# Openings of both gather streams in a two-block transformer kernel: the first head's gates and dots at once, the rest of the opening beside the picks

## The reference, cut to what matters

```python
x = x + g1 * y
h = rmsnorm(x, norm_ffn[layer]) * (1.0 + sc2) + sh2
x = x + g2 * peer_ffn(h, w_q, sub_keys, u, v)

def peer_ffn(h, w_q, sub_keys, u, v):
    q = (h @ w_q).reshape(T, 8, 2, 128)               # 8 heads, two halves each
    s = einsum('thpd,pnd->thpn', q, sub_keys)         # 128 keys per half
    top_s, top_i = top_k(s, 16)
    cand_s = top_s[:, :, 0, :, None] + top_s[:, :, 1, None, :]
    cand_i = top_i[:, :, 0, :, None] * 128 + top_i[:, :, 1, None, :]
    best_s, best_j = top_k(cand_s.reshape(T, 8, -1), 16)
    experts = take_along_axis(cand_i, best_j)         # 8 x 16 = 128 rows per token
    gates = softmax(best_s)
    act = gelu(einsum('cd,ced->ce', h, u[experts]))   # a dot of h with each row of u
    return einsum('ce,ced->cd', gates * act, v[experts])
```

## Time and profile before

| what | us |
|---|---|
| median of 3 runs | 2341.18 |
| the runs | 2337.76 to 2343.08 |
| the profiled execution | 2340.63 |
| its span | 2338.9 |

### The profile page before, as it was taken

The page is one execution under the profiler, slowest core; times in us unless marked ns, Lnnn a source line. Parts: engine busy times, 40 slices in busy tenths (PEclk is TensorE's granted clock), DMA queues, the critical chain, the costliest instruction groups (busy, mean ns, idle before and its releaser), DMA issues. The chain is left out here.

```text
span 2338.9 us, 24802 instructions
## 1 busy us (share of the span) xinstructions
PE 1892.6 (81%) x9231; PEld 1014.7 (43%) x9231; DVE 1337.5 (57%) x3278; ACT 326.9 (14%) x822; POOL 556.5 (24%) x568
## 2 busy tenths in 40 slices
PE   6998666666679799998877777799999988777776
PEld 4665333333357464444333222375655443232222
DVE  3633000000055658768877876657587678778866
ACT  1052000000021420110000000123310100000001
POOL 1000000000000114443434343200144444344332
PEclk9999888888889899999999999999999999999999
DMA  9987999999997369999999999897599999999997
GB/s 399 424 261 279 429 428 429 429 431 429 426 327 325 144 272 372 421 421 421 421 418 415 421 413 422 354 374 294 206 405 422 421 421 419 421 418 421 410 421 321
DMA packets 119160, 894.80 MB, mean 383 GB/s; under 512 B 18460, under 2 KB 30588, under 8 KB 31868
## 3 DMA queue, kind: packets, MB, share of 16 engines
q0 software_dynamic: 73728, 536.90, 55.5%
q1 hardware_dynamic: 45308, 356.25, 37.5%
HBM read 889.68 MB, written 3.42 MB: 382 GB/s over the span
## 5 line engine op out<-in xcount | busy, mean ns | idle before, releaser
L2038 PE MATMUL psum<-sb_area 128*128 128x512 f32 x2048 | 978.5, 615 | 233.5 <-DVE sb_area L2793 229.3
L2819 DVE CUSTOM_DVE_ANT_0 sb_area<-sb_area 128x1024 f32<-128x1024 f32 x512 | 626.1, 1224 | 273.0 <-DMA sb_area<-in_peer_uv,sb_peer_e 270.5
L852 POOL DMA_INDIRECT sb_area<-in_peer_uv,sb_peer_e x512 | 538.8, 1052 | 999.0 <-PE psum L2038 718.7
L2038 PEld LDWEIGHTS psum<-sb_area 128*128 128x128 f32 x2048 | 375.0, 193 | 715.8 <-DVE sb_area L2793 369.1
L1688 PE MATMUL psum<-sb_area 128*32 128x256 f32 x2048 | 172.3, 510 | 130.6 <-DMA sb_area<-in_moe_w_gu 128.0
L2321 DVE COPY sb_area<-psum 128x128 f32<-128x128 f32 x32 | 9.3, 292 | 392.0 <-PE psum L1700 392.0
L1270 ACT ACTIVATE sb_small<-sb_small 128x2 f32<-128x2 f32 x258 | 52.5, 203 | 1140.5 <-DVE sb_small L2819 1140.5
L2793 DVE SCALAR_TENSOR_TENSOR sb_area<-sb_ident,sb_small,sb_area 128x128 f32<-128x128 f32 x512 | 156.7, 347 | 50.2 <-ACT sb_small L1270 45.5
L1387 PE MATMUL psum<-sb_area 128*128 128x256 f32 x784 | 175.3, 385 | 3.5 <-DVE sb_area L2155 3.2
L1688 PEld LDWEIGHTS psum<-sb_area 128*32 128x32 f32 x2048 | 82.6, 145 | 219.6 <-DMA sb_area<-in_moe_w_gu 142.5
L829 POOL TENSOR_SCALAR_AFFINE_SELECT sb_area<-sb_area 128x256 f32<-128x256 f32 x1 | 0.4, 406 | 728.0 <-DVE sb_area L2625 728.0
(11 more groups left out here) (376 smaller groups left out, 1370.2 us busy)
## 6 DMA issues: line engine op xcount, KB each, us to landing
sb_area<-in_moe_w_gu SPq DMA_DIRECT2D x30, 4096.0 KB, 33.5
sb_area<-in_ada_w SPq DMA_DIRECT2D x72, 1024.0 KB, 12.3
sb_area<-in_moe_w_dn SPq DMA_DIRECT2D x32, 2048.0 KB, 24.1
sb_area<-in_peer_w_q_runs SPq DMA_DIRECT2D x8, 2048.0 KB, 10.0
sb_area<-in_sb_w_in_runs SPq DMA_DIRECT2D x6, 2048.0 KB, 19.7
sb_area<-in_odd_w_in_runs SPq DMA_DIRECT2D x6, 2048.0 KB, 11.4
sb_area<-in_even_w_in_runs SPq DMA_DIRECT2D x5, 2048.0 KB, 12.0
sb_area<-in_moe_w_gu SPq DMA_DIRECT2D x4, 2048.0 KB, 20.7
```

The lines of the kernel that those rows point to most:

```text
L852: pool.indirect_dma_start(uv_rows[s], None, rows, bass.IndirectOffsetOnAxis(ap=peer_e[:, m:m + 1], axis=0)).then_inc(named(f"uv_loaded{s}" ...
L2038: last = pe.matmul(ps[:, 4 + 2 * t + half, :], diag[:, m % RING, :], uv_rows[s][:, D + half * HALF:D + (half + 1) * HALF], start=(k == 0), ...
L2819: dve.tensor_tensor_reduce(uv_rows[s][:, 0:D], uv_rows[s][:, 0:D], h_tok[:, m // P, :], 1.0, 0.0, ALU.mult, ALU.add, dots[:, m % BODY:m % ...
```

## The change

Both layers now open in the same way, by one list of places:

- `find_picks` for head 0 is followed by the gates of head 0 alone, and the dots begin. Head 1 makes 5 steps before the first dot (`OPENING_STEPS`) and two steps after each dot up to pick 11, its gates after that.
- The second tile's norm moves beside the picks in `peer0` too, as it was in `peer1`: square sums on ACT after the gelus of pick 3, the variance at pick 5, the root at pick 7, the transposes at pick 8, `low_rows` at pick 10.
- Group 1's products for tile 0 stand behind the `weigh`s of picks 0 to 3, a quarter behind each, and group 0's for tile 1 at picks 12 to 19. Everything behind them moves by 4 picks.
- The keys are turned between the first two products of group 0, and the first key scores stand earlier. The output projection's remaining products stand behind the second part of the key scores in `peer1`, and before the turned tokens in `peer0`.
- Seven slots are used in the first 28 picks of both layers. The eighth joins at pick 28.
- In the whole stream a search now starts at pick 12 of a unit (14 in the first) and makes two steps per dot for the first eight picks, then one; the exponential of its gates stands at pick 22 instead of 26.
- Gates and their sums lie in other memory, and `peer1` has its own diagonal matrices for the first 8 picks.

```diff
-SEARCH_AT = 8
-EXP_AT = 26
-PROJECT_AT = {2: 2, 3: 36}
+OPENING_STEPS = 5
+OPENING_PICKS = 12
+NEXT_SEARCH_AT = 14
+SEARCH_AT = 12
+SEARCHED_AT = 20
+EXP_AT = 22
+PROJECT_AT = {3: 40}
+VAR_AT = 5
+ROOT_AT = 7
+SECOND_AT_PICK = 8
+LOW_ROWS_AT = 10
+FIRST_AT_PICK = 12
+QUICK_AT = 24
...
-        AHEAD = 21
-        slots = [m % RING for m in range(T)]
-        slots += [m % (RING - 1) if m < AHEAD else (m - AHEAD - 1) % RING for m in range(T)]
+        AHEAD = 28
+        slots = [m % (RING - 1) if m < AHEAD else (m - AHEAD - 1) % RING for m in range(T)] * 2
...
 # PE, peer
                 tile_products(0, 0, 0, range(KC // 2, KC))
+                turn_keys()
                 tile_products(0, 0, 1, range(KC)).then_inc(named("head_projected"), 1)
...
+                else:
+                    out_products(*first_out, 1, range(6, 7))
+                    key_scores(0, 0, range(2))
+                    out_products(*first_out, 1, range(7, KC)).then_inc(proj_done, 1)
                     out_products(*last_out, 1, range(KC)).then_inc(proj_done, 1)
+                turn_tok(0)
+                turn_tok(1)
+                if not split:
                     pe.wait_ge(proj_out, head - 1)
-                    tile_products(0, 0, 2, range(KC))
...
+                tile_products(0, 0, 2, range(KC))
+                tile_products(0, 0, 3, range(KC)).then_inc(named("head_projected"), 1)
+                key_scores(0, 0, range(2, GQ))
+                if split:
+                    out_products(*first_out, 1, range(1, KC)).then_inc(proj_done, 1)
+                    out_products(*last_out, 1, range(KC)).then_inc(proj_done, 1)
...
                     weigh(m)
+                    if m < 4:
+                        if m == 0:
+                            pe.wait_ge(w_loaded[ring_of[second]], w_turns(second))
+                        if m == 2:
+                            pe.wait_ge(proj_out, head)
+                        last = tile_products(1, 0, m, range(KC))
+                        if m == 3:
+                            last.then_inc(named("head_projected"), 1)
...
 # DVE, peer
                 for _ in find_picks(0, 0, 1):
                     pass
-                if split:
+                if not split:
                     residual_part(stage, 0, 1)
-                else:
-                    second_tile(stage)
-                for _ in find_picks(0, 1, 1):
+                first_gates = gates(0, 0, 1, 1)
+                next(first_gates)
+                if not split:
+                    residual_closed()
+                others = second_head()
+                for _ in range(OPENING_STEPS):
+                    next(others)
+                for _ in first_gates:
                     pass
...
-                    if m % UNIT == SEARCH_AT and m // UNIT + 1 < UNITS:
+                    if m == NEXT_SEARCH_AT or m > UNIT and m % UNIT == SEARCH_AT and m // UNIT + 1 < UNITS:
                         others = search(m // UNIT + 1)
                     next(others, None)
+                    if m < OPENING_PICKS or (m < NEXT_SEARCH_AT + SEARCHED_AT - SEARCH_AT if m < UNIT else m % UNIT < SEARCHED_AT):
+                        next(others, None)
```

More of the change, by code:

```diff
@@ L2778, in gates, with second_head, residual_closed @@
                     marked()
+                def second_head():
+                    yield from find_picks(0, 1, 1)
+                    yield from gates(0, 1, 1, 8)
+                def residual_closed():
+                    residual_part(stage, 1, 1)
+                    dve.wait_ge(named("x_quarters"), 4 * (TILED[stage] + 1))
+                    dve.sem_inc(x_parts, 2)
+                    dve.sem_inc(x_done, 1)
                 def search(u):
```

217 lines of the change are left out of this document (87 added, 130 removed).

## The result

The changed kernel takes 2361.7 us (median of 5, 2356.9 to 2369.2), the kernel before 2341.2 (2337.1 to 2344.6) beside it: 20.5 us slower by the medians, and a ratio of 1.0096 (95% interval 1.0081 to 1.0111) formed over all the runs; the quotient of the medians is 1.0088. The forecast was 2347, with 2336 to 2354 as its range. Slower was right, the size was not.

A forecast was written before the change was run, and what follows sets the result against it. It took serial gather transfers, 2.48 us a pick, as the bound. Openings of -1 (peer0) and +0.5 (peer1) and later searches of +6.6 gave +6.1 us on 2340.63; with the median 0.5 above that execution it said 2347, range 2336 to 2354.

The forecast's parts named there:

- The bound: Both gather streams: transfers one after another, 2.48 us a pick; other engines count only where POOL issues gathers too late.
- DVE's lateness in a burst: Eight picks with two search steps per dot: DVE falls up to 5.7 us behind, 8.1 with the residual.
- The cover: With eight slots POOL may be 13.4 - 6.8 = 6.6 us late before anything is lost; with seven, 4.1.
- the hidden bursts: Rival for the later searches: the dense bursts cost 0 to 1 us, no change in all, 2341; chance 31%.
- From DVE's lateness to POOL's: Later bursts: DVE's 5.7 us was set directly against POOL's cover of 6.6, so just hidden by 0.9.
- The residual's unit: Unit from pick 128, burst at picks 140 to 147: the residual makes it 8.1 us late, costing 2.5 per layer.
- The bursts at 44, 76 and 108 at zero: These dense searches cost nothing: PE has projections beside them, and the cover leaves 0.9 us.
- PE in the opening of peer0: First four picks: weighing plus product take 3.5 us a pick against 2.48, with a slow clock; 3.1 us lost.
- the sign of being right (943 to 947): Opening of peer0: pick 30 at 943 to 947 would show the forecast right; 945 was forecast.
- The dense search with seven slots: Second search, from pick 14: 1.9 us more lost in peer0; in peer1 the same loss as before.
- The opening of peer1: Engines start 0.8 us later, moved work hides behind transfers, search loses the same as before: +0.5 us (-2 to +2).
- every burst loses: Rival: slow clock in each burst and a floor nearer 8 us, +14 and over, total 2355; chance 13%.

The follow-up runs named there:

- experiments 1: Changed kernel with the searches of the units from pick 128 on spread again, one step per dot from pick 8: 2349.6 us.
- 7: Changed kernel with the first tile's residual after pick 160 instead of 144, out of the dense search's burst: 2356.7 us.
- 6c: Changed kernel with zero matmuls on PE, sized to its gaps, ahead of the weighings of picks 12, 14 and 16 of a unit: 2357.5 us.
- experiment 3: Changed kernel with the four query products moved: in peer0 ahead of the first weighing, in peer1 behind weighings 0 and 1: 2357.7 us.
- Experiment 9: Changed kernel with products moved, softer second search, later searches thinned or spread, and peer1's residual halves one dot earlier: 2337.8 us.

## Why the prediction was wrong, step by step

- **The bound: right.** Where time is lost, it is transfers that run dry because POOL issues late; where POOL is less late (experiments 1, 3 in peer0, and 7), it comes back.
- **DVE's lateness in a burst: right.** 5.7 and 8.1 us forecast; 5.4 to 6.4 in the changed kernel's ten bursts without the residual and 8.2 and 8.3 in the two with it.
- **The cover: this step failed.** "5.7 is under 6.6: with eight slots such a burst is just hidden, by 0.9 us." The 6.6 were 13.4 - 6.8, a median less a minimum, and the minimum was of the 64 landings that the trace has. Set against the gathers' largest lateness, the losses were 3.9 (at 10.4 us late), 2.8 (8.6), 1.8 (7.8), 2.1 (6.6) and 1.4 (6.3). At 10.4 the rule is exact (3.8); near the edge it says 0 where 1.4 to 2.1 are lost. A smaller minimum makes the rule worse, not better: with 5.5 us it would promise 7.9 us of cover. Landings of 6 us do occur, but in the profiles that record all of them never with more than two gathers still ahead (after a stage's first gather), so the minimum already belongs to an almost empty queue and to lost time. Over all profiles, no unit whose gathers stayed within 4.7 us of their pace lost more than 1.1 us, and nearly every one beyond 5.5 us did lose, 0.4 us at least (the lateness of dot 24 picks on). The forecast had the evidence for it: landings near 6.8 "go with lost time" stood there against the hidden bursts, and was then used for their chance and not for the cover. The Trainium skill's rule ("DMA: Bandwidth & Descriptors", section "Anatomy of one DMA — SWDGE (gpsimd) path") gives an estimate of 4.4 us for such a gather. The traces do not agree: the shortest in any profile took 5.3 us. By it the cover would have been 9 us, further off than mine.
- **From DVE's lateness to POOL's: this failed too.** "5.7 is under 6.6" sets DVE's lateness against a cover that is POOL's. Between them stand the diagonals of a pair and PE. In the changed kernel's ten bursts without the residual the gathers were up to 5.4 to 8.5 us late, and in six of them over 6.6, so that by the forecast's own rule they were not hidden; with the residual it was 10.4 in both layers. In 6c, with PE at 2.4 GHz, the four bursts without the residual came to 6.2 to 6.6 and still lost 0.4 to 2.3 us, so that the cover fails by itself as well.
- **The residual's unit: right.** +2.5 per layer forecast, +3.5 and +2.4 measured from pick 138 to 170; experiment 7 takes 2.8 and 2.5 of it away. That the number came out is partly luck: its cover was too large, and the gathers were 2 us later than DVE, which was left out.
- **The bursts at 44, 76 and 108 at zero: wrong, with the cover.** From pick 42 to 138 the drift grew from 3.4 to 5.9 us in peer0 and from 1.3 to 6.5 in peer1. Nor do PE's projections fill its gaps: it stood 4.03 us in the burst at 76 and 4.45 in that at 108, with the granted clock at 1.2 GHz after both (peer0). It was also one of the forecast's signs of being wrong, and it came.
- **PE in the opening of peer0: right.** 3.1 us forecast, 3.6 taken back by experiment 3; 1.7 for the slow clock, 3.69 - 1.88 = 1.8 measured. The first dot came at 861.7, not 865.0, since this execution reached the stage 3 us earlier: 26.9 us after its start, where 27.1 were forecast. For the same reason dot 30, at 944.33, lies within the sign of being right (943 to 947) by luck: from the start of the stage it is 109.5 us, and the forecast's 945 was 107.1.
- **The dense search with seven slots: too cheap**, the same fault as the cover. 1.9 us in peer0 and nothing in peer1 were forecast; thinning it out gave 2.9 and 2.7, and that is not all of it, since 1.8 and 3.1 of drift remain from pick 10 to 30, where the kernel before has 0.2 and 0.8. Up to pick 10 peer0's opening gained 6.4 us, more than the hole's 5.3; it gave all of it back before pick 30 and became +1.4 instead of -1.
- **The opening of peer1: +5.2 instead of +0.5.** The engines start about 0.8 us later after the start of the stage, as forecast, and dot 6 comes 0.5 later (48.9 against 48.4); but dot 10 is 0.4 earlier than before. So the whole +5.2 arises from dot 10 to 30, and the terms that failed are the two that were put at nothing there. One is the dense second search, "I take the same loss": the three kernels with the softer one have dot 30 at 112.0 to 113.5, the seven with the changed opening at 113.5 to 117.1. The other is "PE and DVE have time for the moved work, so that its 1.8 us a pick hide behind the transfers": the weights, now behind the gathers, delay the data of picks 2 and 3, weighing 2 and its product start only at 1703, and gather 9 goes out 3.8 us later than before. How much this second one costs is not shown. Experiment 9 brought gather 9 forward by 6.8 us and dot 30 by 1.5, no more than the scatter. A kernel that issues the weights earlier was not tried. (The terms as written add up to +0.8; nothing in the forecast accounts for the other -0.3.)

The rival "every burst loses" (2355) came nearest. Its "+14 and over" for the bursts met the 13.6 by a slip: 4.5 and five times 1.0 to 1.5 per layer are 19 to 24 us in both layers, which with the openings' -0.5 would be 2360 to 2364. Its floor "nearer 8 us" was near the mark (8 to 9), its slow clock the smaller part of the cause.

## What to carry to other kernels

The cover of a transfer queue is not the median latency less the smallest: look for the landings at which waiting dots first lose their pace, and count from there. Here that was 8 to 9 us of 13, which leaves 4 to 5 us and not 6.6. Compare it with the lateness of the engine that issues the transfers, not with that of an engine ahead of it. See over how many transfers a minimum was taken before building on it. An opening is judged where it ends and not at its first pick: peer0's was 6.4 us ahead at pick 10 and 1.4 behind at pick 30. Work moved out of an opening has to go somewhere, and when it is squeezed into later stretches it is paid there once per unit; two short runs, one that undoes it and one that does it alone, show that price at once. When a load is moved behind others on shared engines, ask first whose data it now delays.
